# A two-block kernel in split fp32: output gates projected beside the attention, fewer operations in an attention head, one modulation vector computed earlier

## The reference

```python
sh_m, sc_m, gt_m, sh_f, sc_f, gt_f = split(silu(c) @ w_mod + b_mod, 6)        # six modulation vectors of 2048
csh_m, csc_m, *_ = split(silu(c_ctx) @ w_mod + b_mod, 6)                      # the context needs the first two
h_lat, h_ctx = rms_norm(x, g) * (1 + sc_m) + sh_m, rms_norm(ctx, g) * (1 + csc_m) + csh_m
p_lat, p_ctx = h_lat @ w_in, h_ctx @ w_in
# eight recurrence heads of 128, forward and backward, starting from the context's state
o = rms_norm(ol_f + ol_b, norm_g) * silu(g_l)                                 # g_l: the output gates, 8 x 128 columns of p_lat
# eight attention heads of 128, two key heads
q, k = rope(rms_norm(q, q_g)), rope(rms_norm(k, k_g))
s = q @ [k_lat, k_ctx].T * 128**-0.5 + mask                                   # 256 x 512 for one head
probs = softmax([s, sink])[..., :-1]
x = x + gt_m * (concat([o, probs @ v]) @ w_out)
x = x + gt_f * swiglu(rms_norm(x) * (1 + sc_f) + sh_f)
```

## Time and profile before

| | |
|---|---|
| median of 3 runs | 3611.9 us (3607.03 to 3613.27) |
| the profiled execution, time | 3611.78 us |
| its span in the trace | 3610.0 us |
| mean granted TensorE clock | 0.977 of full speed |
| PE busy | 3466.7 us, 96% |
| DVE busy | 2414.1 us, 67% |
| ACT busy | 1555.8 us, 43% |
| POOL busy | 172.7 us, 5% |
| read from HBM | 725.98 MB, 202 GB/s over the span |

### The profile page before, as it was taken

One profiled execution on the slowest core, in us unless ns is written; L12 is line 12 of the kernel. 1 busy time (PEld: TensorE's weight loads), 2 busy tenths in 40 slices (PEclk: granted clock), 3 DMA queues, 4 the chain that ended last, 5 costly groups with the idle time before them and its releaser, 6 DMA issues.

```text
span 3610.0 us, 58459 instructions
## 1 busy us (share of the span) xinstructions
PE 3466.7 (96%) x24888; PEld 3200.9 (89%) x24888; DVE 2414.1 (67%) x2995; ACT 1555.8 (43%) x2184; POOL 172.7 (5%) x328
## 2 busy tenths in 40 slices
PE   7889999999999989999999989999988999999999
PEld 3477788699999989999998968888987899999999
DVE  6777666466777676778777466777697666445544
ACT  2244554443433344433334444555454444334443
POOL 0000000000000000000000001000000000000000
PEclk9999999999999999999999999999999999999999
DMA  7632224478887767778776647555553577565565
GB/s 284 235 117 72 83 96 134 154 242 272 275 280 262 255 228 258 259 250 268 245 244 210 183 145 251 175 181 177 176 181 118 176 260 263 179 188 186 186 185 177
DMA packets 201428, 731.90 MB, mean 203 GB/s; under 512 B 22352, under 2 KB 22608, under 8 KB 200656
## 3 DMA queue, kind: packets, MB, share of 16 engines
q1 hardware_dynamic: 153792, 551.20, 45.5%
q0 software_dynamic: 46656, 171.99, 15.3%
q10 hardware_dynamic: 720, 4.98, 0.3%
HBM read 725.98 MB, written 2.10 MB: 202 GB/s over the span
## 4 chain that ended last, share of the span: by engine, by line
PE 86%; DVE 9%; ACT 3%; issue 2%; DMA 1%; ACTq 0%; DVEq 0%
PE ps L859 85%; DVE t L1702 4%; DVE wlo L1771 2%; ACT whi L1348 1%; DVE hT L1702 1%; PE ps L1024 1%; DVE t L2240 0%; DMA res<-in_xT 0%; DVE res L1702 0%; DVE t L2278 0%; DVE t L1880 0%; DVE hT L2044 0%; DMA t<-in_w_ada 0%; DVE hT L2010 0%; DVE t L2001 0%
## 5 line engine op out<-in xcount | busy, mean ns | idle before, releaser
L859 PE MATMUL ps<-hT,whi 128*128 128x256 f32 (+1 forms) x11360 | 2205.6, 294 | 0.0
L859 PEld LDWEIGHTS ps<-hT,whi 128*128 128x128 f32 x11360 | 1797.4, 189 | 59.7 <-issue 6.5
L859 PE MATMUL ps<-hT,wlo 128*128 128x256 f32 (+1 forms) x5680 | 1711.5, 301 | 53.3 <-DVE wlo L1771 19.2
L1771 DVE TENSOR_TENSOR wlo<-raw,whi 128x1024 fp32r<-128x1024 f32 (+1 forms) x990 | 1191.1, 1206 | 820.4 <-ACT whi L1348 818.8
L1348 ACT ACTIVATE whi<-raw 128x1024 fp32r<-128x1024 f32 (+1 forms) x990 | 1029.2, 1042 | 929.8 <-PE ps L859 925.2
L859 PEld LDWEIGHTS ps<-hT,wlo 128*128 128x128 f32 x5680 | 1076.4, 190 | 110.8 <-issue 72.8
L859 PE MATMUL ps<-t,whi 128*128 128x256 f32 x3136 | 562.7, 282 | 0.0
L1702 DVE SCALAR_TENSOR_TENSOR t<-t,misc 128x1024 f32<-128x1024 f32 (+1 forms) x488 | 542.6, 1139 | 18.9 <-DMA t<-in_w_mod 13.7
L859 PEld LDWEIGHTS ps<-t,whi 128*128 128x128 f32 x3136 | 484.6, 190 | 0.4
L859 PE MATMUL ps<-t,wlo 128*128 128x256 f32 x1568 | 446.2, 285 | 5.9 <-DVE wlo L1771 5.9
L859 PEld LDWEIGHTS ps<-t,wlo 128*128 128x128 f32 x1568 | 297.7, 190 | 7.1 <-DVE wlo L1771 4.9
(11 more groups left out here) (213 smaller groups left out, 1579.3 us busy)
## 6 DMA issues: line engine op xcount, KB each, us to landing
raw<-in_w_in_s SPq DMA_DIRECT2D x250, 512.0 KB, 4.7
t<-in_w_mod POOLq DMA_DIRECT2D x192, 512.0 KB, 4.8
raw<-in_w_ffn_gu SPq DMA_DIRECT2D x176, 512.0 KB, 5.1
raw<-in_w_gu SPq DMA_DIRECT2D x176, 512.0 KB, 4.5
t<-in_w_ada POOLq DMA_DIRECT2D x128, 512.0 KB, 5.3
t<-in_w_ada_s SPq DMA_DIRECT2D x64, 512.0 KB, 4.7
raw<-in_w_out SPq DMA_DIRECT2D x64, 512.0 KB, 4.5
raw<-in_w_ffn_down SPq DMA_DIRECT2D x64, 512.0 KB, 4.2
```

What stands on the lines that cost most here:

```text
L859: return e.matmul(o, l, r, start=start, stop=stop)
L1771: tt(lo[:, 0:n], S.buf("raw", p)[:, 0:n], hi[:, 0:n].bitcast(F32), ALU.subtract).then_inc(*up("lo", p))
```

## The change

- Vector (1, 2) is computed as `back` of the first feed-forward, behind (1, 0) and (1, 1). The pace there goes from 5.9 to 4.7. The recurrence stage keeps (1, 3) and (1, 4).
- The eight output gate projections `hgg` move out of the recurrence stage. Each now follows `aq` of the head with the same number. At its evacuation ACT takes the silu, DVE multiplies (L2233 after), ACT rounds into `hT[0]` and DVE subtracts into `hT[1]` (L2235). `at_in` only loads its tables.
- The 16 tiles `out2a` stand behind all of `aq` and `hgg`; `EARLY` is gone. `pace[0]` of the stage goes from 1.4 to 1.6, and at most two raw queries wait instead of three.
- In a head of attention the two halves share one maximum and one chain of small operations (two columns each). ACT multiplies by one over the sum (L1679 after) instead of DVE. The result is read from PSUM by ACT and DVE, without DVE's copy.

```diff
 def before0():
-        s.pace[:] = [3.0, 5.9]
+        s.pace[:] = [3.0, 4.7]
...
             yield from mods(s, 1, [0, 1])
+            yield from mods(s, 1, [2])
...
-    s.back = mods(s, 1, [2, 3, 4])
+    s.back = mods(s, 1, [3, 4])
...
         s.lin("hq", h, [("w_in2_s", h)], T)
-        s.lin("hgg", h, [("w_in2_s", 32 + h)], T)
         s.jobs.append(hgrn(h))
...
-    s.turns, s.pace[0] = True, 1.4
+    s.turns, s.pace[0] = True, 1.6
     for h in range(8):
-        while len(raw) == 3:
+        while len(raw) == 2:
...
-        for m in range(sum(EARLY[:h]), sum(EARLY[:h + 1])):
-            if m == 0:
-                s.need(1, 2)
-            s.lin("res", ("out2a", m), [("w_out_2", m, 0)], T)
+        s.lin("hgg", h, [("w_in2_s", 32 + h)], T)
+    for m in range(16):
+        s.lin("res", ("out2a", m), [("w_out_2", m, 0)], T)
...
             S.free("ps", t, by=("hg_a", "gg", h))
+            g.wait_ge(*at("hg_v", "gated", h), *done_of("vtok", 0))
+            fn(hT[0][:, h, CTX], cat[:, h, :], ACT.Copy).then_inc(*up("at_a", "cat", h))
...
-                g.wait_ge(*at("at_v", "max", h, i))
-                fn(sc, sc, ACT.Exp, bias=o[:, b + 1:b + 2], accum_out=o[:, b + 2:b + 3]).then_inc(*up("at_a", "p", h, i))
-                fn(o[:, b + 3:b + 4], snk, ACT.Exp, bias=o[:, b + 1:b + 2]).then_inc(*up("at_a", "sink", h, i))
+            g.wait_ge(*at("at_v", "max", h))
+                fn(sc[:, i, :], sc[:, i, :], ACT.Exp, bias=o[:, 2 + i:3 + i], accum_out=o[:, 4 + i:5 + i]).then_inc(*up("at_a", "p", h, i))
+            fn(o[:, 6:8], o[:, 2:4], ACT.Exp, bias=sm("attn_sink_2", h, 1)).then_inc(*up("at_a", "sink", h))
+            yield
+                g.wait_ge(*at("at_v", "inv", h))
+                fn(sc[:, i, :], sc[:, i, :], ACT.Copy, scale=o[:, 10 + i:11 + i]).then_inc(*up("at_a", "pn", h, i))
...
-            stt(rsh, S.buf("o", h)[:, 0:T], sm("hg_norm_g_2"), rsh, ALU.mult, ALU.mult).then_inc(*up("hg_v", "on", h))
-            tt(cat[:, h, :], rsh, S.buf("gg", h), ALU.mult).then_inc(*up("hg_v", "cat", h))
+            stt(cat[:, h, :], S.buf("o", h)[:, 0:T], sm("hg_norm_g_2"), rsh, ALU.mult, ALU.mult).then_inc(*up("hg_v", "cat", h))
+        def ev_hgg(t):
+            tt(cat[:, h, :], cat[:, h, :], S.buf("gg", h), ALU.mult).then_inc(*up("hg_v", "gated", h))
+            tt(hT[1][:, h, CTX], cat[:, h, :], hT[0][:, h, CTX].bitcast(F32), ALU.subtract).then_inc(*up("at_v", "cat", h))
...
-                ts(sc[:, i, :], sc[:, i, :], o[:, b + 4:b + 5], None, ALU.mult).then_inc(*up("at_v", "p", h, i))
...
-            e.tensor_copy(sc[:, 0, 0:T], S.buf("ao", h)[:, 0:T]).then_inc(*up("at_v", "o", h))
```

More of the change, by code:

```diff
@@ L735, in program @@
     amask = carve3(2, 512)
-    rawq = ring(3, lambda: carve(T), f6)
+    rawq = ring(2, lambda: carve(T), f6)
     way_sc, way_pT = [], []
@@ L1567, in ev_hgg @@
             S.take(evg, "gg", h)
-            S.free("gg", h, by=("hg_v", "cat", h))
+            S.free("gg", h, by=("hg_v", "gated", h))
             g.wait_ge(*done(t), *S.freed("gg", h))
@@ L1637, in at_in @@
             e.dma_start(amask.rearrange("p t n -> p (t n)"), A["amask"]).then_inc(*up("am_in", n=16))
-            for h in range(8):
-                g.wait_ge(*at("hg_v", "cat", h), *done_of("vtok", 0))
-                fn(hT[0][:, h, CTX], cat[:, h, :], ACT.Copy).then_inc(*up("at_a", "cat", h))
         def ev_aq(t):
@@ L2276, in attend @@
                 S.free("s", h, i, by=("at_v", "s", h, i))
[L2277 to L2280 removed]
+            g.wait_ge(*at("at_v", "s", h, 1))
+            e.tensor_reduce(o[:, 0:2], sc, AX.X, ALU.max).then_inc(*up("at_v", "max0", h))
+            g.wait_ge(*at("at_v", "max0", h))
+            ts(o[:, 2:4], o[:, 0:2], snk, -1.0, ALU.max, ALU.mult).then_inc(*up("at_v", "max", h))
             yield
[L2282 to L2289 removed]
+            g.wait_ge(*at("at_a", "sink", h))
+            tt(o[:, 8:10], o[:, 4:6], o[:, 6:8], ALU.add).then_inc(*up("at_v", "den", h))
+            g.wait_ge(*at("at_v", "den", h))
+            e.reciprocal(o[:, 10:12], o[:, 8:10]).then_inc(*up("at_v", "inv", h))
             yield
@@ L2302, in dve @@
                     "merge": merge, "ev_res": ev_res, "ffn_in": ffn_in, "ev_up_f": ev_up_f, "ctx2": ctx2, "norm2": norm2,
-                    "hg_in": hg_in, "hg_gates": hg_gates, "hgrn": hgrn, "at_in": at_in, "keys": keys, "attend": attend,
+                    "hg_in": hg_in, "hg_gates": hg_gates, "hgrn": hgrn, "ev_hgg": ev_hgg, "keys": keys, "attend": attend,
                     "end": M.fence})
```

51 lines of the change are left out of this document (18 added, 33 removed).

## The result

| | before | after |
|---|---|---|
| median | 3612.59 us (3607.03 to 3615.46, 4 runs) | 3643.47 us (3640.75 to 3644.33, 4 runs) |
| ratio | | 1.0085, 95% interval 1.007 to 1.01 |
| span of the profiled execution | 3610.0 us | 3641.1 us |
| mean granted clock | 0.977 | 0.973 |

The change made the kernel 31 us slower. The forecast was 3597 us, faster with a chance of 0.71, in a range of 3582 to 3614. It was wrong in sign and the time is outside the range.

The account below looks back on a forecast made before the run. PE was taken as the bound, busy 96%, with room mainly in the attention stage. 3611.8 - 22.7 (attention) + 3 (recurrence) + 2 (first feed-forward) + 2.5 (context norm) gave 3597 us, range 3582 to 3614.

Parts of the forecast that it names:

- Step 1: Attention stage, output gates moved in and `out2a` behind them: idle 10 us instead of 26.7, gain 22.7 us (14 to 33).
- the keys' start: Attention stage: the keys still wait for two inverses, but DVE has less in front of it; 4 us idle.
- 7 bare segments, 3 taken: Attention stage: seven segments without products between them cost 4.9 us at most; 3 us taken, since products stand close behind.
- 3 us for all heads: Attention stage: ACT waits for a joint maximum before both exponentials; 3 us idle over all heads, ends 0 and 10.
- The last term of the sum: Attention stage: clock lost on PE's busy time falls from 10 to 4 us.
- the waits move to ACT: Rival, attention stage: joint maximum, normalisation and gates' rounding hold ACT, splits come late, 14 us on top; 3611, chance 0.15.
- Step 2: Recurrence stage: less cover exposes 2.8 us at three boundaries between heads, 8 us at most; cost 3 us.
- Step 3: First feed-forward: 32 more accumulations make DVE full while small backlogs stay hidden; cost 2 us, ends 0 and 21.
- DVE is exactly full: First feed-forward: a step with two accumulations takes 4.98 us of DVE against 4.97 of PE, for 16 of 17 steps.
- My test for this step: First feed-forward: PE's waits for `wlo` above 10 us before 1900 us would prove the cost of 2 us wrong.
- DVE is the bound of the first feed-forward: Rival, first feed-forward: double steps take full durations, 21 us of PE waits, context norm 6; 3628, slower, chance 0.11.
- the third rival's threshold: First feed-forward: DVE as bound decides once a step stalls over 0.34 us beyond the forecast's 2 us in all.

Follow-up runs that it names:

- the run at 2.8: The changed kernel with one number changed, the pace of the recurrence's segments 2.8 instead of 3.2: 3630.04 us, ratio 1.0049.
- the run at 2.4: The changed kernel with the pace of the recurrence's segments at 2.4 instead of 3.2: 3629.78 us, ratio 1.0053.

## Why the prediction was wrong, point by point

**Step 1, the attention stage: gain 22.7, measured 12.6, and for another reason.** I explained the idle time by the segments without products between them, and let it fall with their number. The runs split the gain: 17.5 us from the vector (three kernels gave 17.5, 17.5 and 17.7), 1.0 from the gates, -5.1 from the slim heads; the sum is 13.4, measured 12.6. It is not a clean split: the run with the gates alone holds ten accumulations more. But for the keys' start the vector's share was not in my sum: the 19 accumulations stood in DVE's load, 82% to 65%, and I called neither engine a bound. The failed step is "7 bare segments, 3 taken" and "3 us for all heads": they cost 5.7 and, as waits for `wlo`, 5.2 us, and a place I had not listed, the first `out2a` behind the last gate, 3.9. The keys' start was right, 3.8 us for 4. The last term of the sum failed too: the lost clock on busy time was to fall from 10 to 4 us, and it fell from 9.6 to 8.7. (A small slip besides: laid out as beats, the old order has 16 segments in its last bare place, not 17.) Products between segments do not remove a chain's waiting; when all bare places were taken out, in after and in before, the waits kept their sum within some 3 us and the stage its length within 1.2. DVE's load was right: 134 us by the window, 131 forecast, ACT 127 against 130. The rival "the waits move to ACT" fits the slim heads.

The eight extra table loads take 10.3 us with 0.1 us idle before them:

```profile
L1570 ACT ACT_TABLE_LOAD x8 | 10.3, 1283 | 0.1
```

The 1.38 us of drain that the Trainium skill (ScalarE: Activation LUTs, What ACT_TABLE_LOAD costs) adds for each would be 11 us more on ACT. This trace does not show them.

**Step 2, the recurrence stage: cost 3, measured 24.3. This is the largest error.** The mechanism and the places were right (three boundaries with 3 blocks, waits before the transposes of every second head). The sizes were not. I summed the chain's instructions to 6.7 us and took the difference to what lies there, 2.8 us at three places, then shaved it to 3 in all. The trace has 2.2 to 2.8 us at these places, 7.4 in all, near the 8 I then took for an upper end. Two terms were missing: three waits of 2.5 us where the end of a head now meets the next head's gates, and the lower clock, 8 us for the stage in after and nothing in after without the vector, with the same products and segments. The run with boundaries of 4 blocks and all products in place (17.4 us) shows that the spacing of the segments does most of it without any product moved, the run at 2.8 that spreading the cover returns 10.9, and the run at 2.4 that closer spacing only moves the heads' ends onto the gates. The even spacing still costs 13.4 us (in two kernels): 8.6 us more idle time and 1.7 us of clock at 2.8, and 3 us which no run here settles.

**Step 3, the first feed-forward: cost 2, measured 15.8; five kernels with the vector at pace 4.7 had 11.5 to 15.8.** The sum, 4.98 us of DVE against 4.97 of PE, was right to see the stage as full. The step that failed is "DVE is exactly full": DVE's idle time for `whi` in the earlier trace rows was taken as free, and PE lost 10.9 us while DVE still stood 26.8 of 300 us for `whi`. Some 2 us of the 15.8 are the sum of the moved vector, which my sum had in neither stage. The bound lies between pace 4.7 (10.9 us lost without any more work) and 5.4 (2.4 lost, within the scatter). My test for this step, waits for `wlo` above 10 us before 1900, did not fire at 6.9 us in the list of waits, nor did DVE reach 90%: both tests were too blunt, since more than half of the loss shows as busy time of PE. The context norm cost 3.6, forecast 2.5.

**The rivals.** "DVE is the bound of the first feed-forward" had the sign, and nearly the size there (19.4 us with the norm, against 27), but no rival had the recurrence stage. With it at 24.3 instead of 3 my sum would have been 3618, with feed-forward and norm as measured 3633, and with 12.6 instead of 22.7 in the attention stage 3643. (In the third rival's threshold the forecast's gain stands as 14.7 us; its own terms give 15.2, which changes 0.34 to 0.35 us and nothing else.)

## What to carry to other kernels

Before products are moved out of a stage that shows no wait, lay out where each chain's end and start fall then: a wait of zero says that the cover sufficed, not by how much, and an end that lands on the next chain's start holds up all that is queued behind both. Idle time of an engine within a producer loop (PE frees, ACT rounds, DVE splits) need not be free time: here PE lost 10.9 us with DVE at 84 to 85%, and nothing that can be told at 82%. Run the parts of a change alone: here one part was worth 17.5 us in one stage and cost 16 in others, and one number (the pace of the steps with two accumulations) turned it into a gain.

## What the runs showed that I had not expected

- In the attention stage 19 accumulations of 1.28 us, 24.3 us of work on an engine at 82%, were worth 17.5 us of time; 3.7 of them were the vector's sum on PE, which moved with it.
- A stretch of 300 us with PE busy for 294.4 us held 102 matmuls fewer than one with 300; the count told of 12 us, the idle time of 5.6 and the clock of 5.1. At pace 4.7 alone, with the same work and the same lost clock, a stage 10.9 us longer shows 6.0 of them as busy time of PE.
- PE idled 16.4 to 16.9 us in the recurrence stage of three kernels with the same products and segments there, and its lost clock was 28.6, 27.2 and 20.1 us (20.5 before, with 1.2 us idle). Two waits of 2.51 us were followed by a clock of 0.61 and of 1.00. So the clock cannot be charged by the idle time: it cost 8 us in one of these kernels and nothing in another.
